# A two-layer hybrid mixer on one core: gates, first taps and modulation vectors moved between the input projection's chunks

## The chip, the cores and the metric

The kernel runs on one core of a Trainium2 chip. The metric is the device time of one execution in microseconds (us), here as the median of several runs. One core has five engines with an instruction stream each: TensorE (PE, matrix products; PEld is its weight load), VectorE (DVE), ScalarE (ACT), GpSimd (POOL) and SyncE (SP), whose queue issues most of the DMA loads. An engine takes its instructions in the order in which they are written, and waits on semaphores for the others.

## The reference, cut to what matters

256 context tokens and 256 latent tokens of width 1024 go through two layers. The part of a layer that the change touches:

```
mod = silu(c) @ w_mod[l] + b_mod[l]        # six vectors of 1024: sh1, sc1, gt1, sh2, sc2, gt2
h = rms_norm(x) * (1 + sc1) + sh1
a_val, a_gate, s_bg, s_cg, s_x, c_x, c_g = split(h @ w_in[l])       # 2304 columns
ya = silu(layer_norm(conv31(a_val * sigmoid(a_gate))))              # 256 channels
yb = s_bg * conv3(s_cg * s_x)                                       # 256 channels
xc = conv4(c_x) + lru_conv_b                                        # 512 channels
for d in (forward, backward):
    r = sigmoid(xc @ w_a[d] + b_a[d]); i = sigmoid(xc @ w_x[d] + b_x[d])
    log_a = 8 * r * log_sigmoid(lam[d])
    h_d = scan(exp(log_a), sqrt(1 - exp(2 * log_a)) * i * xc)
yc = (h_f + h_b) * gelu(c_g)
x = x + gt1 * (head_rms_norm([ya, yb, yc]) @ w_out[l])
x = x + gt2 * channel_mixer(...)            # layer 0: SwiGLU, layer 1: 2 of 8 SwiGLU experts
```

In layer 1 the context tokens are needed for `c_x` alone (for the scans' first states).

## The kernel before, in words

Activations lie transposed, channels on the partitions and the 512 tokens (layer 1: mostly the 256 latent ones) along the free axis. A product in fp32 accuracy is made of three products of a high and a low part: ScalarE copies a weight chunk of 1 MB into its high part (`hi`, L1464), VectorE takes the difference (`low`, L1896), and TensorE multiplies high by high, high by low and low by high.

`w_in` comes in nine chunks of 256 columns, in the order `WIN_ORDER` (0, 1, 4, 3, 2, 5, 6, 7, 8); this document calls them first to ninth chunk. Chunks 5 and 6 (sixth and seventh) are `c_x`, chunks 7 and 8 (eighth and ninth) are `c_g`. The third-next chunk's `hi` and `low` are made when a chunk's product ends.

After the ninth chunk comes what is called the interior here: the gates of the linear recurrence (RG-LRU), four tiles of 128 channels in each of two directions. Per tile TensorE makes two products of 512 columns (`bank<-xc,G`), ScalarE runs `gates(d, t)` (two tanh, exp, tanh, and outside the forward direction of layer 0 a square, L1611 to L1624), VectorE four or three operations (L2179 to L2188), ScalarE a square root (L1659), VectorE a product and a scan (L2209 to L2222). Between them stand the layer norm of the 31-tap convolution (its centring is L2196, its squares on ScalarE L1651) and the head norms (L1629 to L1640). Then the output projection `w_out` follows.

A modulation vector takes four chunks of `w_mod` of 1 MB and is read by TensorE straight from the ring buffer `raw` (`modulation`, 32 instructions, `bank<-raw,cc`). Before, all four vectors of a layer (gt1, sh2, sc2, gt2) are made in the interior. VectorE copies each out by `mod_row`.

The order of the work is written out by hand. Who does how many of the 62 taps of the 31-tap convolution when (L2059 first taps, L2062 the others) stands in the table `TAPS`; `CONF_AT` and `MEAN_AT` say after which gate tile the centring and the mean come. The DMA order is the list `CHUNKS`: the ring has five slots, so a chunk is loaded when the one five places before it has been used (a projection chunk: when its `low` is done). `mods_after` puts the `w_mod` chunks into that list.

At the start, small tables of parameters (`TABLES`) are transposed by TensorE into a bank and copied to `PT`, and `decay_rates` makes 8 log_sigmoid(lam) by 22 small operations on VectorE.

Of the kernel before, what the change touches and what calls it, by code (L numbers as in the profile page):

```python
# [29 lines left out]
P = 128  # L30
D = 1024
KD = D // P
NC = 256
# [181 lines left out]
def program(nc, a, out, known, marks):  # L215
# [5 lines left out]
    with ctx:  # L221
# [165 lines left out]
        MOD, STAT = bank[6], bank[7]  # L387

# [59 lines left out]
        def weights(c):  # L448
# [11 lines left out]
            if c[0] == "down":  # L460
# [12 lines left out]
        TAPS = {0: {"half": 2, 1: 8, 4: 13, 3: 11, 2: 13, 5: 4, 7: 11, 8: 0, "gate": 0},  # L473
                1: {"half": 3, 1: 3, 4: 5, 3: 7, 2: 21, 5: 0, 7: 4, 8: 7, "gate": 4}}
        BACK = (5, 6, 2, 3)

        CONF_AT = {0: 1, 1: 3}
        MEAN_AT = {0: 1, 1: 4}

        def mod_rows(l, q):  # L480

            b, half = {(0, 2): (4, 0), (0, 3): (4, 1), (0, 4): (5, 0), (0, 5): (5, 1),
                       (1, 0): (6, 1), (1, 1): (7, 0), (1, 2): (4, 0), (1, 3): (4, 1), (1, 4): (5, 0),
                       (1, 5): (5, 1)}[l, q]
            return bank[b][:, 256 * half:256 * half + 256]

# [283 lines left out]
        def _(pe):  # L770
# [10 lines left out]
            def tables(n):  # L781

                _, rows, _ = TABLES[n]
                return nc.tensor.transpose(STAT[:, P * n:P * n + rows], rows_sb[0:rows, n, :], ident[0:rows, 0:rows])
# [105 lines left out]
            def quarter_rows(c4):  # L890

                pe.wait_ge(dve_done, at("xT", "in", 4 + c4 % 2))
# [22 lines left out]
            def started():  # L915
# [7 lines left out]
                quarter_columns(0)  # L923
                for k in range(KD - 2):
# [19 lines left out]
                for t in range(2):  # L944
# [3 lines left out]
                    if t == 0:  # L948
                        pe.wait_ge(table_in, 16 * sum(len(parts) for parts, _, _ in TABLES[1:]))
                        pe.wait_ge(dve_done, at("t", 0, 1, KD - 1))  # L950
                        for m in range(1, len(TABLES)):
                            i = tables(m)
                        i.then_inc(pe_done, pe_n("tables"))
# [25 lines left out]
            for l in range(2):  # L979
# [7 lines left out]
                for c in WIN_ORDER[2:]:  # L987
                    project(("w_in", l, c), slice(0, T) if c in (5, 6) else ts, None)
                pe.wait_ge(gate_in, 8 * 16 * (l + 1))
                for q in range(8):  # L990
# [3 lines left out]
                    if q < 2:  # L994
                        pe.wait_ge(*evacuated(("w_in", l, WIN_ORDER[6 + q])))
                    else:
                        pe.wait_ge(act_done, at("gate_read", l, q - 2))
                    for w in range(2):
                        i = mm(bank[2 * (q % 2) + w][:, :], G[:, 8 * d + 4 * w + t, :], xc[:, t, :], True, True)
                    i.then_inc(pe_done, pe_n("gate", l, q))  # L1000
                    if (l, q) == (1, 3):
                        modulation(*MIX_MODS[l][0][0])
                    if q == CONF_AT[l]:
                        head_sums(l, ts, HEAD_SUM[0], (2, 3))
# [6 lines left out]
                    if (l, q) == (1, 4):  # L1011
                        modulation(*MIX_MODS[l][0][1], range(2))
                    if (l, q) == (0, 3):
                        modulation(*MIX_MODS[l][0][0])
# [9 lines left out]
                    if q == 5:  # L1024
                        modulation(*MIX_MODS[l][0][1], range(2 * l, MOD_K))
# [6 lines left out]
                modulation(*MIX_MODS[l][1][0])  # L1032
# [421 lines left out]
        def _(act):  # L1454
# [60 lines left out]
            for l in range(2):  # L1515
                ts = slice(lo[l], T)
                if l == 0:
# [25 lines left out]
                    for c4 in range(QUARTERS):  # L1543
# [5 lines left out]
                        if c4 == 0:  # L1549
                            hi(1)  # L1550
                    hi(2)
# [5 lines left out]
                for t in range(2):  # L1557
# [5 lines left out]
                    if l == t == 0:  # L1563
                        act.wait_ge(dve_done, at("lam_abs"))
# [1111 lines left out]
```

## Time and profile before

| what | us |
|---|---|
| three runs | 1555.26, 1559.27, 1558.04 |
| median | 1558.04 |
| the profiled execution | 1560.56 |
| its span | 1558.8 |
| its mean granted TensorE clock | 0.977 |
| busy: TensorE, VectorE, ScalarE | 1476.8, 838.1, 619.1 |

The page of the profile gives, of one execution, each engine's busy time and the span in 40 slices. The span is the time from the first to the last instruction; the profiled execution took 1.8 us more than its span. Because the engines' roles change from stage to stage, the shares of the whole span say little about one stage. The rows below are therefore read by stretch. Layer 0's first products start at 24.34 us, its ninth chunk ends near 135 us, its `w_out` starts at 188.81 us; layer 1's projection runs from 630 to 696 us and its `w_out` starts at 748.51 us. The experts fill the time from about 800 us on.

### The profile page before, as it was taken

The numbers are of one execution on the slowest core, as the hardware profiler recorded it, in microseconds if no ns is written. First come the engines' busy times: TensorE is split into PE (matmuls) and PEld (weight loads), VectorE is DVE, ScalarE is ACT, GpSimd is POOL, SyncE is SP. The second block draws the span as 40 slices with busy tenths as digits, with TensorE's granted clock in tenths as the row PEclk, the third lists the DMA queues.
The fourth block names the chain that finished last, engine by engine and source line by source line (L and its number), as shares of the span: only waits on it lengthen the run. The fifth ranks groups of instructions, "written<-read, shape, count | busy, mean of one in ns | idle before, by whom it ended". The sixth has DMA issues, their size and how long they took to land.

```text
span 1558.8 us, 21878 instructions
## 1 busy us (share of the span) xinstructions
PE 1476.8 (95%) x8674; PEld 1041.6 (67%) x8675; DVE 838.1 (54%) x1139; ACT 619.1 (40%) x702; POOL 18.2 (1%) x60
## 2 busy tenths in 40 slices
PE   6999698999999999896989999999999999999996
PEld 4886486788888887883855576565756566555754
DVE  4799944333333333898564554445645555445552
ACT  4426723232122232549253433434443444434442
POOL 2000000000000000000000000000000000000000
PEclk8999999999999999899989999999999999999998
DMA  9734914822543234349069999989999999999992
GB/s 330 228 108 163 350 60 158 216 61 75 135 109 91 74 92 135 109 135 347 6 266 389 341 327 332 342 329 401 385 408 405 404 384 402 408 356 402 384 409 88
DMA packets 214152, 395.47 MB, mean 254 GB/s; under 512 B 12044, under 2 KB 131232, under 8 KB 214048
## 3 DMA queue, kind: packets, MB, share of 16 engines
q1 hardware_dynamic: 213456, 393.80, 70.7%
q8 instruction: 74, 1.21, 0.3%
q10 hardware_dynamic: 592, 0.21, 0.1%
q14 instruction: 30, 0.25, 0.0%
HBM read 392.93 MB, written 1.05 MB: 253 GB/s over the span
## 4 chain that ended last, share of the span: by engine, by line
PE 84%; DVE 6%; ACT 5%; DMA 3%; issue 2%; DVEq 0%; SPq 0%; ACTq 0%
PE bank L772 82%; DMA raw<-in_moe_w 2%; DMA raw<-in_w_mod 1%; PE bank L1301 1%; ACT w_hi L1738 1%; DVE w_lo L2370 1%; DVE tb L1913 1%; ACT la L1617 1%; DVE lr L2222 1%; DVE y L2062 0%; DVE h_lo L1921 0%; ACT lr L1611 0%; PE bank L1246 0%; ACT lm L1659 0%; DVE li L2209 0%
## 5 line engine op out<-in xcount | busy, mean ns | idle before, releaser
L2370 DVE TENSOR_TENSOR w_lo<-raw,w_hi 128x2048 fp32r<-128x2048 f32 x132 | 302.4, 2291 | 266.2 <-ACT w_hi L1738 263.3
L1738 ACT ACTIVATE w_hi<-raw 128x2048 fp32r<-128x2048 f32 x132 | 252.3, 1912 | 406.2 <-PE bank L772 275.4
L772 PE MATMUL bank<-h_hi,w_hi 128*128 128x512 f32 (+1 forms) x768 | 285.7, 372 | 14.1 <-DVE h_lo L1921 12.0
L772 PE MATMUL bank<-h_lo,w_hi 128*128 128x512 f32 (+1 forms) x768 | 282.7, 368 | 0.0
L772 PE MATMUL bank<-h_hi,w_lo 128*128 128x512 f32 (+1 forms) x768 | 282.5, 368 | 0.0
L1464 ACT ACTIVATE w_hi<-raw 128x2048 fp32r<-128x2048 f32 (+1 forms) x64 | 113.7, 1776 | 195.7 <-PE bank L772 192.8
L772 PEld LDWEIGHTS bank<-h_hi,w_hi 128*128 128x128 f32 x768 | 146.7, 191 | 41.1 <-DVE h_lo L1921 13.9
L772 PEld LDWEIGHTS bank<-h_hi,w_lo 128*128 128x128 f32 x768 | 146.7, 191 | 23.8
L772 PEld LDWEIGHTS bank<-h_lo,w_hi 128*128 128x128 f32 x768 | 147.0, 191 | 23.0
L1896 DVE TENSOR_TENSOR w_lo<-raw,w_hi 128x2048 fp32r<-128x2048 f32 (+1 forms) x64 | 135.9, 2123 | 38.6 <-ACT w_hi L1464 38.5
L772 PE MATMUL bank<-w_hi,hc_hi 128*128 128x512 f32 (+1 forms) x384 | 153.6, 400 | 2.9 <-ACT warm L1793 2.9
L772 PE MATMUL bank<-w_lo,hc_hi 128*128 128x512 f32 (+1 forms) x384 | 144.7, 377 | 0.0
L772 PE MATMUL bank<-w_hi,hc_lo 128*128 128x512 f32 (+1 forms) x384 | 144.0, 375 | 0.0
L772 PE MATMUL bank<-raw,hcs 128*64 128x512 f32 (+2 forms) x736 | 116.7, 453 | 0.1
L772 PEld LDWEIGHTS bank<-w_hi,hc_hi 128*128 128x128 f32 x384 | 72.5, 189 | 48.3 <-issue 24.3
L2279 DVE TENSOR_TENSOR sq<-tb,bank 128x512 f32<-128x512 f32 x22 | 15.1, 687 | 125.3 <-ACT tb L1704 125.3
L772 PEld LDWEIGHTS bank<-w_hi,hc_lo 128*128 128x128 f32 x384 | 72.6, 189 | 14.3
L772 PEld LDWEIGHTS bank<-w_lo,hc_hi 128*128 128x128 f32 x384 | 72.7, 189 | 10.5
L772 PEld LDWEIGHTS bank<-raw,hcs 128*64 128x64 f32 x736 | 43.6, 137 | 48.8 <-issue 43.3
L1704 ACT ACTIVATE tb<-bank 128x512 f32<-128x512 f32 x22 | 13.1, 597 | 155.5 <-PE bank L772 155.5
L772 PE MATMUL bank<-w_hi,hd_hi 128*128 128x512 f32 x176 | 72.6, 412 | 0.0
L772 PE MATMUL bank<-w_lo,hd_hi 128*128 128x512 f32 x176 | 69.3, 394 | 0.0
(323 smaller groups left out, 1795.7 us busy)
## 6 DMA issues: line engine op xcount, KB each, us to landing
raw<-in_moe_w SPq DMA_DIRECT2D x220, 1024.0 KB, 9.4
raw<-in_w_mod SPq DMA_DIRECT2D x48, 1024.0 KB, 8.6
raw_x<-in_moe_w SPq DMA_DIRECT2D x44, 1024.0 KB, 9.4
raw<-in_ffn_w SPq DMA_DIRECT2D x44, 512.0 KB, 5.4
raw<-in_w_in SPq DMA_DIRECT2D x18, 1024.0 KB, 5.7
raw<-in_ffn_w SPq DMA_DIRECT2D x16, 704.0 KB, 4.8
raw<-in_w_out SPq DMA_DIRECT2D x8, 1024.0 KB, 5.5
x_in<-in_ctx SPq DMA_DIRECT2D x1, 1024.0 KB, 5.0
```

The costliest lines, as they stand in the source:

```text
L772: return nc.tensor.matmul(dst, lhsT, rhs, start=first, stop=last)
L1301: i = nc.tensor.transpose(bank[TURN_BANK][:, P * t:P * t + P], hid[:, p % 2, P * t:P * t + P], ident[:, :])
L1464: nc.scalar.activation(w_hi[:, s % SPL, 0:n], raw[:, POS[c] % RAW, 0:n], ACT.Copy)\
L1617: nc.scalar.activation(la[:, t, :], lr[:, t, :], ACT.Exp, scale=cln[:, k:k + 1], bias=cln[:, k:k + 1]).then_inc(act_done, act_n())
L1704: nc.scalar.activation(tb[:, i11 % 2, :], bank[2 * (s % 3)][:, :], ACT.Silu)\
L1738: nc.scalar.activation(w_hi[:, j % SPL, :], raw[:, E_SLOT[j], :], ACT.Copy)\
L1896: V.tensor_tensor(w_lo[:, s % SPL, 0:n], raw[:, POS[SPLIT[s]] % RAW, 0:n], w_hi[:, s % SPL, 0:n].bitcast(F32), ALU.subtract).then_inc(dve_ ...
L1913: i = V.scalar_tensor_tensor(tb[:, d % 2, tok(s)], xT[:, d, tok(s)], amp[:, l, w - 1, d, s:s + 1], STAT[:, tok(s)], ALU.mult, ALU.mult)
L2222: V.tensor_tensor_scan(lr[:, t, tok(s)][:, ::-1], la[:, t, tok(s)][:, ::-1], li[:, t, tok(s)][:, ::-1], lr[:, t, 0:1] if s else 0.0, ALU.m ...
L2279: V.tensor_tensor(sq[:, i11 % 2, :], tb[:, i11 % 2, :], bank[2 * (s0 % 3) + 1][:, :], ALU.mult)\
L2370: V.tensor_tensor(w_lo[:, j % SPL, :], raw[:, E_SLOT[j], :], w_hi[:, j % SPL, :].bitcast(F32), ALU.subtract).then_inc(dve_done, dve_n(name ...
```

## The change

It does these things, in both layers unless a layer is named:

- the tables are transposed before the first product, into bank 4, and copied and turned into decay rates by VectorE between the first quarters of the input (layer 0);
- ScalarE makes the first tap of three convolutions (`conf_tap` for one of two tiles, `sconv_tap`, `lru_tap`), which VectorE made before;
- modulation vectors gt1 and sh2 (numbers 2 and 3) are made after the fourth and after the fifth chunk instead of in the interior, and their `w_mod` chunks stand at those places in the DMA order; number 4 moves to where they were;
- the gates of tiles 0 and 1 of the forward direction are made by TensorE between the two halves of the eighth and of the ninth chunk, and ScalarE's and VectorE's part of them follows there; they use other buffers (`lru`);
- the tables `TAPS`, `CONF_AT` and `MEAN_AT` change: no tap is left for the time after the ninth chunk's product in layer 0, ten are left in layer 1; layer 0's mean and centring come after the fourth gate tile instead of the second.

The core of the diff:

```
 def mods_after(c):
+    if c[0] == "w_in" and c[2] in WIN_ORDER[2:4]:
+        l, q = MIX_MODS[c[1]][0][WIN_ORDER.index(c[2]) - 2]
+        return [(l, q, kq) for kq in range(MOD_K)]
     if c[0] == "w_in" and c[2] == WIN_ORDER[-1]:
-        return [(l, q, kq) for batch in MIX_MODS[c[1]] for l, q in batch for kq in range(MOD_K)]
+        return [(l, q, kq) for l, q in MIX_MODS[c[1]][1] for kq in range(MOD_K)]
...
-        TAPS = {0: {"half": 2, 1: 8, 4: 13, 3: 11, 2: 13, 5: 4, 7: 11, 8: 0, "gate": 0},
-                1: {"half": 3, 1: 3, 4: 5, 3: 7, 2: 21, 5: 0, 7: 4, 8: 7, "gate": 4}}
+        TAPS = {0: {"half": 2, 1: 11, 4: 13, 3: 16, 2: 16, 5: 4, 7: 0, 8: 0, "gate": 0},
+                1: {"half": 3, 1: 3, 4: 5, 3: 9, 2: 21, 5: 2, 7: 9, 8: 10, "gate": 0}}
-        CONF_AT = {0: 1, 1: 3}
-        MEAN_AT = {0: 1, 1: 4}
+        CONF_AT = {0: 3, 1: 3}
+        MEAN_AT = {0: 3, 1: 4}
...
                 quarter_columns(0)
+                pe.wait_ge(table_in, 16 * sum(len(parts) for parts, _, _ in TABLES[1:]))
+                for m in range(1, len(TABLES)):
+                    i = tables(m)
+                i.then_inc(pe_done, pe_n("tables"))
...
-                for c in WIN_ORDER[2:]:
+                for c in WIN_ORDER[2:7]:
                     project(("w_in", l, c), slice(0, T) if c in (5, 6) else ts, None)
+                    if c in WIN_ORDER[3:5]:
+                        if c == WIN_ORDER[3]:
+                            pe.wait_ge(dve_done, at("t", l, 1, KD - 1))
+                        modulation(*MIX_MODS[l][0][WIN_ORDER.index(c) - 3])
                 pe.wait_ge(gate_in, 8 * 16 * (l + 1))
-                for q in range(8):
+                for q, c in enumerate(WIN_ORDER[7:]):
+                    w, banks = take(("w_in", l, c))
+                    for t in range(2):
+                        for kk in range(KD):
+                            o = 256 * kk + P * t
+                            i = split_mm(banks[t][:, ts], (w[0][:, o:o + P], w[1][:, o:o + P]),
+                                         (h_hi[:, kk, ts], h_lo[:, kk, ts]), kk == 0, kk == KD - 1)
+                        if t:
+                            i.then_inc(pe_done, pe_n("mm", ORD["w_in", l, c]))
+                        elif q == 0:
+                            pe.wait_ge(dve_done, at("xc", l, 0))
+                            pe.wait_ge(*evacuated(("w_in", l, WIN_ORDER[6])))
+                            gate(0)
+                        else:
+                            pe.wait_ge(dve_done, at("xc", l, 1))
+                            pe.wait_ge(dve_done, at("mod_row", *MIX_MODS[l][0][1]))
+                            gate(1)
+                for q in range(2, 8):
...
                 for c in WIN_ORDER[2:]:
                     s = ORD[("w_in", l, c)]
                     b = bank[2 * (s % 3):2 * (s % 3) + 2]
+                    if c == 7:
+                        act.wait_ge(dve_done, at("clp"))
+                        gates(0, 0)
+                    if c == 8:
+                        gates(0, 1)
+                        gelu(7)
                     act.wait_ge(pe_done, at("mm", s))
                     hi(s + SPL)
+                    if c == 8:
+                        gelu(8)
...
+                    if c in (5, 6):
+                        act.wait_ge(act_done, act_n.n)
+                        for t in (2 * (c - 5), 2 * (c - 5) + 1):
+                            nc.scalar.activation(xc[:, t, :].rearrange("p (s w) -> p s w", s=2), cxp[:, t, :, 0:256],
+                                                 ACT.Identity, scale=colv("lru_conv_w", 16 * l + t),
+                                                 bias=colv("lru_conv_b", 4 * l + t))\
+                                .then_inc(act_done, act_n("lru_tap", l, t))
...
                     if c in (7, 8):
                         conf_taps(budget[c])
+                        gated_input(0, c - 7)
...
                 for d in range(2):
                     for t in range(4):
                         q = 4 * d + t
+                        if q >= 2:
+                            gated_input(d, t)
```

Three places show how instructions stand. On TensorE in layer 0, before, nothing but `xc,G` gate products stands between the ninth chunk's last product and the head sums (`sq,head_51`), and a whole vector (`raw,cc` x32) comes after the fourth tile:

```order
L772 MATMUL bank<-h_hi,w_lo 128x512
L772 MATMUL bank<-xc,G 128x512 x4
L772 MATMUL bank<-sq,head_51 32x128 x4
L772 MATMUL bank<-sq,head_51 16x128 x4
L772 MATMUL bank<-y,ones_d 128x512 x2
L772 MATMUL bank<-xc,G 128x512 x4
L772 MATMUL bank<-raw,cc 32x256 x32
L772 MATMUL bank<-xc,G 128x512 x2
```

In the changed kernel such a vector stands in the projection, between the last product of the fourth chunk and the first of the fifth (another follows the fifth chunk, and two `xc,G` instructions stand in the middle of the eighth and of the ninth):

```order
L786 MATMUL bank<-h_hi,w_lo 128x512
L786 MATMUL bank<-raw,cc 32x256 x32
L786 MATMUL bank<-h_hi,w_hi 128x512
L786 MATMUL bank<-h_lo,w_hi 128x512
...
L786 MATMUL bank<-h_hi,w_lo 128x512
L786 MATMUL bank<-xc,G 128x512 x2
L786 MATMUL bank<-h_hi,w_hi 128x512
```

Sixty-four `raw,cc` instructions and two gate tiles moved ahead of the ninth chunk's end.

On ScalarE in layer 0, before, the ninth chunk's `w_hi` and gelu (`cxp<-bank`) are followed by all four forward tiles (`lr`, `li`, `la`, `lr`), of which the first is shown:

```order
L1464 ACTIVATE w_hi<-raw 128x2048
L1589 ACTIVATE cxp<-bank 128x2x256 x2
L1611 ACTIVATE lr<-bank,PT 128x512
L1613 ACTIVATE li<-bank,PT 128x512
L1617 ACT_TABLE_LOAD
L1617 ACTIVATE la<-lr,cln 128x512
L1619 ACTIVATE lr<-lr,clp 128x512
```

Now tile 1 stands ahead of them, with its results in `tb`, `sx` and `y`, and the eighth chunk's gelu and its table load stand between:

```order
L1617 ACTIVATE tb<-bank,PT 128x512
L1619 ACTIVATE sx<-bank,PT 128x512
L1623 ACTIVATE y<-tb,cln 128x512
L1625 ACTIVATE tb<-tb,clp 128x512
L1636 ACT_TABLE_LOAD
L1636 ACTIVATE cxp<-bank 128x2x256
L1497 ACTIVATE w_hi<-raw 128x2048
L1636 ACTIVATE cxp<-bank 128x2x256
L1617 ACTIVATE lr<-bank,PT 128x512
L1619 ACTIVATE li<-bank,PT 128x512
L1623 ACT_TABLE_LOAD
```

Two of four tiles are ahead of the last `w_hi` of the projection, and the table load for exp stays in the interior.

On VectorE in layer 0, before, the centring (`y<-bank,y`) stands behind the second tile (whose last two operations are the first two rows) and ahead of the third:

```order
L2185 SCALAR_TENSOR_TENSOR li<-li,xc 128x512
L2188 TENSOR_SCALAR lm<-lm 128x512
L2196 SCALAR_TENSOR_TENSOR y<-bank,y 128x512 x2
L2179 TENSOR_TENSOR lm<-la 128x512
L2183 SCALAR_TENSOR_TENSOR lm<-lm,lr 128x512
```

Now tile 1 stands behind the projection's last `w_lo`, and the centring behind the fourth tile:

```order
L1963 TENSOR_TENSOR w_lo<-raw,w_hi 128x2048
L2188 TENSOR_TENSOR y<-y 128x512
L2192 SCALAR_TENSOR_TENSOR y<-y,tb 128x512
L2193 SCALAR_TENSOR_TENSOR sx<-sx,xc 128x512
L2195 TENSOR_SCALAR y<-y 128x512
...
L2193 SCALAR_TENSOR_TENSOR li<-li,xc 128x512
L2195 TENSOR_SCALAR lm<-lm 128x512
L2266 SCALAR_TENSOR_TENSOR y<-bank,y 128x512 x2
L2276 TENSOR_TENSOR sx<-y,sx 128x512
```

The centring moved behind two more tiles; ScalarE's squares of it still stand ahead of the square roots.

On SP's queue, the eight `w_mod` chunks of vectors 2 and 3 stood behind the first three `w_out` chunks; now four stand between the sixth and the seventh `w_in` chunk, and four between the seventh and the eighth.

## Rows read from the trace of the kernel before

**Rows 1.** Windows, layers 0 and 1: start:end, length, engines busy, clock, DMA, GB/s

```profile
56.14:134.88 78.74, 78.74 (x350) 65.19 (x348) 77.19 (x132) 24.41 (x26) 0.00 (x0) 1.00 0.37 119
134.88:188.81 53.93, 41.46 (x453) 21.69 (x452) 50.17 (x77) 46.22 (x70) 0.00 (x0) 0.94 0.87 308
642.64:696.40 53.76, 53.76 (x361) 49.99 (x362) 48.72 (x77) 23.39 (x27) 0.00 (x0) 1.00 0.43 138
696.40:748.51 52.11, 38.01 (x452) 19.63 (x451) 47.03 (x88) 45.16 (x74) 0.00 (x0) 0.90 0.75 283
715.00:720.00 5.00, 4.42 (x60) 2.06 (x56) 4.90 (x7) 4.53 (x10) 0.00 (x0) 1.00 1.02 407
```

**Rows 2.** Chain of waits, layer 0's interior: start, us, what

```profile
135.16 1.64 ACT w_hi L1464
...
139.22 1.28 ACT L1617
...
147.15 0.57 ACT lr L1611
...
149.71 1.04 ACT sq L1651 x2
...
156.01 0.58 ACT lr L1611
...
188.81 54.77 PE bank L772 x392
```

**Rows 3.** Chain of waits, layer 1's interior

```profile
696.48 1.92 ACT w_hi L1464
...
700.78 2.77 DVE y L2062 x7
...
719.06 0.58 ACT lr L1611
...
722.14 0.57 ACT lr L1611
...
748.51 11.52 PE bank L772 x141
```

**Rows 4.** Timeline of TensorE, layer 0: start, us, instruction, idle before

```profile
134.88 3.60 PE L772 MATMUL bank<-xc,G 128*128 128x512 f32 x8
...
145.21 3.66 PE L772 MATMUL bank<-raw,cc 128*32 128x256 f32 x64
...
157.23 1.07 PE L772 MATMUL bank<-raw,cc 128*32 128x256 f32 x16 [1.23 <-DMA raw<-in_w_mod]
...
176.90 1.13 PE L772 MATMUL bank<-sq,head 128*4 128x128 f32 x16 [7.80 <-ACT sq L1629]
```

**Rows 5.** Timeline of VectorE, layer 0

```profile
120.17 1.91 DVE L2089 TENSOR_SCALAR xc<-cxp,PT 128x512 f32<-128x512 f32 x4
...
144.62 0.69 DVE L2179 TENSOR_TENSOR lm<-la 128x512 f32<-128x512 f32 x1 [0.20 <-ACT lr L1619]
...
146.90 1.28 DVE L2196 SCALAR_TENSOR_TENSOR y<-bank,y 128x512 f32<-128x512 f32 x2
```

**Rows 6.** Timeline of VectorE, layer 1

```profile
709.73 0.69 DVE L2183 SCALAR_TENSOR_TENSOR lm<-lm,lr 128x512 f32<-128x512 f32 x1
...
711.27 1.67 DVE L2062 SCALAR_TENSOR_TENSOR y<-vp,PT,y 128x256 f32<-128x256 f32 x4
...
714.39 0.75 DVE L2196 SCALAR_TENSOR_TENSOR y<-bank,y 128x256 f32<-128x256 f32 x2
```

**Rows 7.** Timeline of ScalarE, layer 1, at the fourth chunk's end

```profile
657.42 1.92 ACT L1464 ACTIVATE w_hi<-raw 128x2048 fp32r<-128x2048 f32 x1 [3.30 <-PE bank L772]
```

**Rows 8.** SP's queue, layer 1, the issue behind the sixth chunk's `low`

```profile
657.31 0.37 SPq L541 DMA_DIRECT2D raw<-in_w_out  x1
```

**Rows 9.** DMA issues in that window: KB each, us to landing

```profile
raw<-in_w_out SPq DMA_DIRECT2D x1, 1024.0 KB, 5.8
```

**Rows 10.** Timeline of TensorE, the first product of layer 0

```profile
24.34 0.80 PE L772 MATMUL bank<-h_hi,w_hi 128*128 128x512 f32 x1 [5.31 <-DVE h_lo L1921]
```

More of the change, by code:

```diff
@@ L993, in _ @@
                         pe.wait_ge(dve_done, at("xc", l, t))
-                    if q < 2:
-                        pe.wait_ge(*evacuated(("w_in", l, WIN_ORDER[6 + q])))
+                    if q == 3:
+                        pe.wait_ge(*evacuated(("w_in", l, WIN_ORDER[7])))
                     else:
                         pe.wait_ge(act_done, at("gate_read", l, q - 2))
[L998 to L1003, printed above, removed]
+                    gate(q)
+                    if q == 3:
+                        pe.wait_ge(act_done, at("gate_read", l, 1))
                         head_sums(l, ts, HEAD_SUM[0], (2, 3))
@@ L1010, in _ @@
                         i.then_inc(pe_done, pe_n("conf_mean", l))
[L1011 to L1014, printed above, removed]
+                    if q == 3 + l:
+                        modulation(*MIX_MODS[l][1][0], range(2))
                     if q == 4:
@@ L1024, in _ @@
                     if q == 5:
-                        modulation(*MIX_MODS[l][0][1], range(2 * l, MOD_K))
+                        modulation(*MIX_MODS[l][1][0], range(2, MOD_K))
                     if q == 6:
@@ new lines, in gelu @@
+                def gelu(c):
+                    act.wait_ge(dve_done, at("xc", l, 3))
+                    s = ORD[("w_in", l, c)]
+                    for t in range(2):
+                        nc.scalar.activation(cxp[:, 2 * (c - 7) + t, lo[l] // NC:2, 2:2 + 256],
+                                             bank[2 * (s % 3) + t][:, ts].rearrange("p (s w) -> p s w", w=256),
+                                             ACT.Gelu_apprx_tanh)\
+                            .then_inc(act_done, act_n(*(("evac", s) if t else ())))
@@ L1641, in head_out @@
                         .then_inc(act_done, act_n("y_hi", l, i8))
[L1643 removed]
                 for d in range(2):
[L1645 removed]
+                    for t in range(2 - 2 * d, 4):
                         gates(d, t)
@@ L1936, in normed @@
                             low(1)
+                            dve.wait_ge(pe_done, at("tables"))
+                            for m in range(1, len(TABLES)):
+                                to_columns(m).then_inc(dve_done, dve_n(*(("PT",) if m == len(TABLES) - 1 else ())))
+                            halved()
+                        if c4 == 1:
+                            decay_rates()
                     low(2)
@@ L2148, in _ @@
                     elif c == 5:
-                        for k in range(SCONV_K):
+                        dve.wait_ge(act_done, at("sconv_tap", l))
+                        for k in range(1, SCONV_K):
                             for t in range(2):
```

185 lines of the change are left out of this document (93 added, 92 removed).

## The prediction

> **What bounds the kernel now.** I read three views in this order. First the windows by stage: in both projections TensorE is busy for the whole stretch, 78.74 of 78.74 us and 53.76 of 53.76, at full clock; in both interiors it is not, 41.46 of 53.93 us and 38.01 of 52.11, while ScalarE and VectorE are busy for nearly all of them [rows 1]. So the reader is to see two regimes that follow each other: TensorE sets the projection's end, ScalarE or VectorE the interior's. Second the chain of waits: it runs through ScalarE from 135.16 us to the end of layer 0's gates [rows 2], and in layer 1 through VectorE's taps at 700.78 us, then through ScalarE [rows 3]. Third the timelines: a modulation vector takes TensorE 3.66 us, two gate tiles 3.60 us, and at 176.90 us TensorE had stood idle for 7.80 us behind ScalarE's squares, although four vectors were made in that interior [rows 4]. Its work there is covered.
>
> **The projections.** The change puts two vectors and two gate tiles in front of the ninth chunk's end: 2 x 3.66 + 3.60 = 10.9 us of TensorE in each layer [rows 4], in the stretch where TensorE never waits [rows 1]. Nothing leaves that stretch, so layer 0's ninth chunk ends at 135.16 + 10.9 = 146.1 us.
>
> In layer 1 a wait on DMA is added. The latent projection's chunks last only 5.8 us each, and the ring makes loads late: the seventh `w_in` chunk used to be loaded far ahead, now its slot comes free with the sixth chunk's `low`, whose issue stands at 657.31 us [rows 8]. A load of that place took 5.8 us to land [rows 9]; alone I take 5, so it lands near 662.3. Its `w_hi`, which started at 657.42 us [rows 7], starts 5 us later. Vector 3's four chunks take the slots of vector 2's, freed from 658.4 on, and queue behind it. At 407 GB/s (the last window of [rows 1]) 1.05 MB take 2.6 us, so they land near 665, 667.6, 670.2 and 672.7. TensorE reaches vector 3 at 657.4 + 3.7 + 5.8 = 666.9 and would end at 670.5; behind the last landing it ends at about 673.3. That is 2.8 us of waiting. Bounds: 0, if transfers overlap as well as the 1.23 us that is layer 0's longest wait for them lets hope [rows 4]; and 10, if each batch is as late as twice a 5.8 us landing. I take 2.8, from the rate. The late seventh and eighth `w_hi` also hold ScalarE and VectorE, but their results are wanted from 684 us on. In layer 0 chunks last 10.9 us and the same sums end before TensorE asks: 0.
>
> **Layer 0's interior.** What leaves ScalarE's chain is two tiles at 149.71 - 147.15 = 2.56 us, 5.1 us [rows 2]. The table load of 1.28 us stays, since gelu stands between. From the ninth chunk's end, `w_hi` and gelu take 2.9 us, so tile 2 starts at 149.0 us, and its decay is ready 4.0 us later, at 153.0; tile 3's at 155.5. Before, the centring ran at 146.90 us, while ScalarE was still in the gates [rows 5]. Now it stands behind VectorE's part of tile 3: 155.6 + 2.28 (144.62 to 146.90 [rows 5]) = 157.9, and its first half ends at 158.5. ScalarE, done at 155.5, waits 3.1 us for it before the squares, and no other work is queued for it except what stands behind: square roots and the whole backward direction. From the squares to the first backward tile it was 156.01 - 149.71 = 6.3 us [rows 2], so that tile starts at 165.0 instead of 156.01: +9.0 us. Behind it nothing on the chain changes, and `w_out` starts near 197.8 instead of 188.81. VectorE's relief (four first taps of `xc` 1.91 us [rows 5], and a few more) lies in the projection, where VectorE isn't waited for, and the taps now ScalarE's lie where ScalarE is busy 24.41 of 78.74 us [rows 1]: 0 either way. Vectors 4 and 5 are made in less crowded interiors: 0.
>
> **Layer 1's interior.** The ninth chunk ends at 696.48 + 10.9 + 2.8 = 710.2. The gates of tile 1 are released only in the middle of that chunk, about 2.9 us ahead of its end; four activations (2.6), a table load and gelu (2.0) keep ScalarE until 711.9, so the last `w_hi` is 1.7 us late and ends at 713.9. VectorE then has `w_lo` (2.3), ten taps at 0.4 us (1.67 for four), tile 1 (2.3, with the square now VectorE's), tiles 2 and 3 at 711.27 - 709.73 = 1.54 us each, and the centring [rows 6]: 713.9 + 2.3 + 4.0 + 2.3 + 3.1 + 0.7 = 726.3. ScalarE is done with tile 3 at 722 and waits for it, as it did before. From the centring's end to the first backward tile it was 719.06 - 715.1 = 4.0 with the second half of the squares inside it; less what overlaps, the tile starts at 729.4 against 719.06: +10.4 us. The 19 taps that VectorE had there before are 10 now, and that with the two tiles of 722.14 - 719.06 = 3.08 us [rows 3] is what buys back 3.3 of the 13.7 us.
>
> **The start.** TensorE had stood idle for 5.31 us before the first product, waiting for VectorE [rows 10]; the three transposes go into that gap, and the table copies and decay rates into gaps in which VectorE waited for the next quarter. Between -0.5 (the transposes no longer stand between products) and +1.5 (the decay rates reach into the next quarter); I take -0.1.
>
> **The sum** against the profiled execution (1560.56 us, which is 2.5 above the median): +9.0 + 10.4 - 0.1 = +19.3 us, so 1579.9 there and 1577.3 on the scale of the median 1558.04. Its ends: with all waits of VectorE and DMA gone, the two tiles fully repaid and layer 1 bound by ScalarE alone, +5.8 and +5.0, together +11; with 10 us of DMA wait in layer 1 instead of 2.8 and some 2 for the start and for the clock, +28.5.
>
> **The clock.** The interiors have a granted clock of 0.94 and 0.90 [rows 1], that is, TensorE fell from 2.4 to 1.2 GHz in the idle time ahead of 176.90 us and came back after it. With one vector less there, that idle time grows from 7.80 to about 13 us [rows 4]. The work that follows until `w_out` is the same and lasts 12 us, in which the clock came back before, so I count 0, with 1 us a layer as the upper bound. The Trainium skill (TensorE: Matmul & The Clock Gate, the part on the clock gate) says that idle gaps throttle the engine and that this penalty is paid again each time. By that rule the added idle is harmful if the clock is still low when `w_out` starts; the trace agrees that it falls, and shows it back in time.
>
> **Rivals.**
> A, the other side: the interior is paced by the stream of `w_mod`. For it: DMA is busy 0.87 of layer 0's interior, and sixteen chunks of 2.6 us are 41 us of 54 [rows 1]. Eight of them leave for a stretch with a share of 0.37. Then each interior shortens by 8 x 2.6 = 20.5 us and each projection grows by 10.9, a gain of 9.6 a layer: 1558 - 19 = 1539. It decides if TensorE's wait for a chunk ends later than ScalarE's squares do. Against it: TensorE waited for a chunk 1.23 us, and 7.80 us for the squares with its vectors done [rows 4]. The Trainium skill (Perfetto Trace Analysis, Optimization Strategy) says that where the most contended engine changes over time, interleaving those regimes may help. That is what the change tries; by this rule the time would fall towards 1539 too, but the rows let only ScalarE's 5 to 6 us a layer be interleaved, while TensorE's work goes into the regime that TensorE bounds.
> B, cancelled: layer 0's centring isn't waited for (CONF_AT costs nothing), layer 1's DMA wait is 0, and VectorE's relief shortens more than ScalarE's chain: under +4.7 us in all. Against it is that even the two chains at their shortest leave +11: 1561.
> C, worse: layer 1's ring is late at every step (seventh chunk, vector 3, eighth chunk), and TensorE stands 10 us or more: 1588. For it is that the loads now follow use and not lie ahead; against it are 10.9 us chunks behind them in which to catch up.
>
> **Chances.** Forecast 0.75 (1568 to 1585); A 0.05; B 0.06; C 0.14. A measurement of this kernel tells about 0.3%, 4.7 us, from no change. So faster 0.05, the same 0.05, slower 0.90. The time is 1577, the range 1567 to 1587.
>
> **What would show it.** Right: in layer 0 the ninth chunk's `w_hi` starts near 146 instead of 135.16, the first backward tile near 165, `w_out` near 198; ScalarE idle some 3 us before the squares; in layer 1 a wait of TensorE for `w_mod` of 2 to 3 us before the sixth chunk, ninth chunk +13.7, `w_out` +10.4 against the layer's own start; TensorE's longest idle time in layer 0's interior 12 to 14 us. Wrong: a projection that grows by less than 10 us, or an interior shorter by more than 8 us, in which case ScalarE was not what set it.

## The result, and the profile after

The changed kernel takes 1582.44 us (median of 4 runs, 1578.33 to 1582.47) where the kernel before takes 1557.94: a ratio of 1.0153 [1.0132, 1.0174]. It is slower, as forecast, by 24.5 us where +19.3 were forecast (1577, range 1567 to 1587). Its profiled execution took 1578.33 us with a span of 1576.6; the other three have spans of 1580.7, and e0 takes up that difference.

The windows of its stages, columns as in [rows 1]: layer 0's projection from a `w_hi` near 56 us to the ninth chunk's, its interior up to `w_out`; then layer 1's projection from the third chunk's end to the ninth's, and its interior. (The projections' windows in [rows 1] begin at other events, 1.7 us earlier in layer 0 and 9 us in layer 1, so their lengths are not to be compared; the table below has both kernels from the same event.)

```profile
56.26:146.11 89.85, 88.90 (x479) 69.39 (x478) 76.20 (x105) 34.29 (x40) 0.00 (x0) 1.00 0.60 206
146.11:197.99 51.88, 33.92 (x317) 17.48 (x315) 42.67 (x62) 40.59 (x62) 0.00 (x0) 0.77 0.45 143
659.59:719.90 60.31, 56.14 (x422) 45.86 (x422) 45.35 (x75) 24.31 (x32) 0.00 (x0) 1.00 0.79 270
719.90:768.34 48.44, 30.09 (x318) 14.91 (x317) 43.22 (x77) 41.05 (x67) 0.00 (x0) 0.82 0.36 122
```

The reader is to see that layer 0's projection has grown by 12.3 us (from the same event, in the table below) and its interior has shrunk by only 2 against [rows 1], although TensorE has 7.5 us less to do there and DMA's share fell from 0.87 to 0.45. TensorE's work left a place where nobody waited for it. In both projections TensorE is now no longer busy all the time: 0.95 us idle in layer 0, 4.2 in layer 1.

The timeline of ScalarE in layer 0's interior, which answers to [rows 2]:

```profile
146.11 1.91 ACT L1497 ACTIVATE w_hi<-raw 128x2048 fp32r<-128x2048 f32 x1 [0.50 <-PE bank L786]
...
154.73 0.81 ACT L1625 ACTIVATE lr<-lr,clp 128x512 f32<-128x512 f32 x1
158.56 1.23 ACT L1718 ACTIVATE sq<-y 128x512 f32<-128x512 f32 x2 [3.02 <-DVE y L2266]
...
164.97 0.67 ACT L1617 ACTIVATE lr<-bank,PT 128x512 f32<-128x512 f32 x1
```

The ninth chunk's `w_hi` starts 10.95 us later than the 135.16 of [rows 2], the gates are done at 155.5, then ScalarE waits 3.02 us for the centring (L2266), and the first backward tile starts at 164.97. TensorE's rows in the two layers, which answer to [rows 4]:

```profile
125.91 1.98 PE L786 MATMUL bank<-xc,G 128*128 128x512 f32 x4 [0.95 <-DVE xc L2169]
138.62 1.88 PE L786 MATMUL bank<-xc,G 128*128 128x512 f32 x4
...
185.93 1.13 PE L786 MATMUL bank<-sq,head 128*4 128x128 f32 x16 [13.81 <-ACT sq L1697]
...
674.43 1.07 PE L786 MATMUL bank<-raw,cc 128*32 128x256 f32 x16
676.39 1.07 PE L786 MATMUL bank<-raw,cc 128*32 128x256 f32 x16 [0.89 <-DMA raw<-in_w_mod]
678.94 1.07 PE L786 MATMUL bank<-raw,cc 128*32 128x256 f32 x16 [1.48 <-DMA raw<-in_w_mod]
681.53 1.07 PE L786 MATMUL bank<-raw,cc 128*32 128x256 f32 x16 [1.52 <-DMA raw<-in_w_mod]
```

The idle time behind the squares has grown from 7.80 us [rows 4] to 13.81. In layer 1 vector 3 waits three times for its chunks, 3.89 us. The loads of `w_in` come late too. The first block below, from ScalarE's timeline, shows the `w_hi` of the seventh and the eighth chunk in layer 1, the first of which answers to [rows 7]. The second, from VectorE's timeline, shows such lateness in layer 0:

```profile
670.08 1.92 ACT L1497 ACTIVATE w_hi<-raw 128x2048 fp32r<-128x2048 f32 x1 [8.05 <-DMA raw<-in_w_in]
684.57 1.92 ACT L1497 ACTIVATE w_hi<-raw 128x2048 fp32r<-128x2048 f32 x1 [12.57 <-DMA raw<-in_w_in]
```

```profile
100.04 2.29 DVE L1963 TENSOR_TENSOR w_lo<-raw,w_hi 128x2048 fp32r<-128x2048 f32 x1 [4.43 <-ACT w_hi L1497]
...
122.47 4.05 DVE L2169 SCALAR_TENSOR_TENSOR xc<-cxp,PT,xc 128x512 f32<-128x512 f32 x6
126.44 2.28 DVE L1963 TENSOR_TENSOR w_lo<-raw,w_hi 128x2048 fp32r<-128x2048 f32 x1
```

The second block is a new feature of layer 0: VectorE stands idle for 4.43 us behind a late load, and then works without a gap until `xc`, for which TensorE waits 0.95 us.

Where the time went is read best by stage. This table, made from the traces of all kernels, has the time between named events: start (to the fourth `w_hi` of the timeline from 40 us on, at the third chunk's end), projection (from there to the ninth chunk's `w_hi`), interior (to the first product of `w_out`), middle (to the same third chunk of layer 1), projection and interior again, and the rest.

| kernel | start | proj. 0 | int. 0 | middle | proj. 1 | int. 1 | rest | ratio to before |
|---|---|---|---|---|---|---|---|---|
| before | 69.88 | 65.28 | 53.65 | 462.85 | 44.82 | 52.03 | 810.29 | |
| changed | 68.50 | 77.61 | 51.88 | 461.60 | 62.15 | 46.60 | 808.26 | 1.0153 [1.0132, 1.0174] |
| changed, again (e0) | 68.93 | 77.13 | 51.72 | 463.14 | 64.80 | 46.59 | 809.39 | 1.0167 [1.0153, 1.0181] |
| e1, vectors back | 69.34 | 74.50 | 51.74 | 462.86 | 50.05 | 46.73 | 808.78 | 1.0054 [1.0042, 1.0067] |
| e2, vectors only | 68.30 | 72.91 | 53.62 | 463.45 | 57.20 | 53.01 | 810.11 | 1.0143 [1.0127, 1.0158] |
| e3, centring early | 68.73 | 77.48 | 49.17 | 461.35 | 64.81 | 46.61 | 808.85 | 1.0145 [1.0131, 1.0160] |
| e4, gates late | 68.07 | 72.91 | 56.84 | 461.32 | 59.54 | 51.11 | 808.91 | 1.0160 [1.0144, 1.0176] |
| e5, e1 + tap table | 68.95 | 68.81 | 51.74 | 461.35 | 50.06 | 46.73 | 809.06 | 1.0007 [0.9998, 1.0016] |
| e6, three mends | 69.70 | 68.81 | 49.17 | 461.20 | 48.48 | 47.84 | 807.30 | 0.9999 [0.9989, 1.0010] |
| e7, layer 1 later | 69.53 | 77.35 | 51.73 | 463.28 | 60.29 | 46.60 | 809.72 | 1.0148 [1.0132, 1.0163] |
| e8, taps and tables | 68.91 | 65.28 | 53.64 | 462.74 | 44.55 | 54.05 | 808.33 | 1.0002 [0.9993, 1.0012] |
| e9, two mends | 69.24 | 68.82 | 49.17 | 463.60 | 50.06 | 46.67 | 809.64 | 0.9997 [0.9988, 1.0006] |

Start, middle and rest vary by 1 to 3 us between executions whatever the kernel. The other four columns repeat within 0.2 us where the code is the same (projection 0 of the changed code within 0.5), except projection 1 of kernels with its vectors early. Differences of 1 us in those four are read as real, smaller ones not.

### The profile page after: what moved, and what is told of

Same layout as the page of the kernel before. It is cut to its first block, busy times and chain, and to the rows that moved or that the text cites. A ratio compares the mean times of both kernels' runs of the same rounds, so it can differ in the third digit from the quotient of the medians.

```text
span 1576.6 us, 21881 instructions
## 1 busy us (share of the span) xinstructions
PE 1482.3 (94%) x8674; PEld 1042.5 (66%) x8675; DVE 834.0 (53%) x1125; ACT 628.6 (40%) x716; POOL 18.2 (1%) x60
## 4 chain that ended last, share of the span: by engine, by line
PE 83%; DVE 8%; ACT 4%; DMA 2%; issue 2%; POOL 0%; DVEq 0%; ACTq 0%; POOLq 0%
PE bank L786 81%; DVE y L2140 2%; DVE w_lo L1963 1%; DMA raw<-in_w_in 1%; PE bank L1334 1%; DMA raw<-in_w_mod 1%; DMA raw<-in_moe_w 1%; ACT w_hi L1497 1%; DVE tb L1980 1%; DVE h_lo L1988 0%; PE bank L1279 0%; PE bank L811 0%; DVE lr L2289 0%; ACT la L1623 0%; DVE y L2280 0%
## 5 line engine op out<-in xcount | busy, mean ns | idle before, releaser
L786 PEld LDWEIGHTS bank<-w_lo,hc_hi 128*128 128x128 f32 x384 | 72.4, 189 | 10.4
```

The source lines that it names most:

```text
L786: return nc.tensor.matmul(dst, lhsT, rhs, start=first, stop=last)
```

## The experiments

In the expectations a theory is what the run should show if my reading is right, and a rival what it should show if another is. The code cuts show the core of each edit; "..." marks what is left out.

**e1: the vectors back.** The rest of the change stays.

```
-    if c[0] == "w_in" and c[2] in WIN_ORDER[2:4]:
-        l, q = MIX_MODS[c[1]][0][WIN_ORDER.index(c[2]) - 2]
...
-                        modulation(*MIX_MODS[l][0][WIN_ORDER.index(c) - 3])
...
+                    if (l, q) == (1, 4):
+                        modulation(*MIX_MODS[l][0][1], range(2))
+                    if (l, q) == (0, 3):
+                        modulation(*MIX_MODS[l][0][0])
...
+                modulation(*MIX_MODS[l][1][0])
```

> The changed kernel with modulation vectors 2 and 3 back in the interiors, at the places of the kernel before; gates of tiles 0 and 1, first taps on ScalarE and early tables stay. Theory (TensorE sets the projection's end, so 2 x 3.66 us per layer are paid there, and layer 1 pays its 3.9 us of waiting for w_mod too): -7.3 in layer 0, less about 2.5 us in which TensorE now waits for VectorE's xc (which was ready at 126.4 us and comes some 5 us earlier without the late load, against TensorE being there at 119), and -7.3 - 3.9 in layer 1: about -16 us, so 1566 where the changed kernel has 1582. TensorE's wait for ScalarE's squares in layer 0's interior falls from 13.8 to 6 to 8 us. Rival A (the stream of w_mod chunks paces the interior): the interiors grow by as much as the projections shrink, or more: 1580 or above. Rival D (VectorE sets layer 0's projection, its taps stand ahead of xc): layer 0 gives back nothing, only layer 1's 11: 1571.

Measured: 1565.31 us beside 1556.20. The interiors didn't move (51.74 and 46.73 us against 51.88 and 46.60) although two vectors each went into them: rival A is dead. Layer 1's projection fell by 12.1 us. TensorE's wait for ScalarE's squares in layer 0 is 6.10 us. Layer 0's projection fell by only 3.1, less than my 4.8, and the timeline of TensorE says why:

```profile
121.92 3.67 PE L783 MATMUL bank<-xc,G 128*128 128x512 f32 x4 [3.74 <-DVE xc L2168]
```

and the windows just before and during that row:

```profile
118.00:121.92 3.92, 0.18 (x1) 0.00 (x1) 3.92 (x7) 0.00 (x0) 0.00 (x0) 1.00 0.00 0
121.92:128.50 6.58, 6.58 (x18) 4.03 (x19) 6.58 (x8) 2.68 (x4) 0.00 (x0) 0.74 0.41 121
```

TensorE waits 3.74 us for `xc`, and then the granted clock is 0.74, that is, the first part of the stretch is at 1.2 GHz: the same four matrix products take 3.67 us and not 1.98. The wait costs 3.7 and the clock behind it 1.7 or more.

**e2: the vectors alone**, on the kernel before.

```
+    if c[0] == "w_in" and c[2] in WIN_ORDER[2:4]:
+        l, q = MIX_MODS[c[1]][0][WIN_ORDER.index(c[2]) - 2]
...
+                        modulation(*MIX_MODS[l][0][WIN_ORDER.index(c) - 3])
...
+                    if q == 3 + l:
+                        modulation(*MIX_MODS[l][1][0], range(2))
```

> The kernel before with one part of the change alone: modulation vectors 2 and 3 made after the fourth and the fifth chunk, their w_mod chunks at that place in the DMA order, vector 4 in their place in the interior. Theory: +7.3 in layer 0, +7.3 and 3 to 4 us of waiting for w_mod in layer 1, nothing back from the interiors: +18, about 1576. Rival A (w_mod paces the interior): 1539 to 1545, below the kernel before. Rival D (VectorE sets layer 0's projection): layer 0 costs less than 7.3, since VectorE was busy 77 of 79 us there: +11 to +14 in all, 1570.

Measured: 1579.50 beside 1556.20, +23 where I expected +18. Projection 0 +7.6, interior 0 unchanged (53.62), projection 1 +12.4 with waits of 4.2 us for `w_mod`, interior 1 +1.0. These four stages sum to +21 us, 3 more than expected, nearly all of it in layer 1. The vectors alone make up nearly the whole loss. That e1, without them, is slower than the kernel before by 9 us all the same comes mostly from the wait for `xc`, which shows only when the vectors are gone (e5). Rival D fell for this kernel: VectorE, 77 of 79 us busy, did not hold the projection.

**e3: the centring early.**

```
-        CONF_AT = {0: 3, 1: 3}
-        MEAN_AT = {0: 3, 1: 4}
+        CONF_AT = {0: 2, 1: 3}
+        MEAN_AT = {0: 2, 1: 4}
```

> The changed kernel with layer 0's mean and centring after the third gate tile instead of the fourth. Theory (ScalarE waited 3.0 us for the centring with all else queued behind the squares): ScalarE goes straight from the gates to the squares, -2.6 us, first backward tile near 162.4 instead of 165.0. Rival (the centring only moved the wait: VectorE's part of the fourth tile, now later by the centring's 1.3 us, holds the square roots, or TensorE is late with the mean): 0 to -1.

Measured: interior 0 is 49.17 us, 2.7 less. The squares' row in the timeline of ScalarE, and the first backward tile:

```profile
156.10 1.23 ACT L1718 ACTIVATE sq<-y 128x512 f32<-128x512 f32 x2 [0.47 <-DVE y L2266]
...
162.51 0.67 ACT L1617 ACTIVATE lr<-bank,PT 128x512 f32<-128x512 f32 x1
```

The wait is 0.47 us where it was 3.02. The median is 3.0 us below e0's 1582.72; the kernel before, run beside each, was 0.7 lower beside e3.

**e4: the gates of tiles 0 and 1 late.**

```
-                        elif q == 0:
-                            pe.wait_ge(dve_done, at("xc", l, 0))
-                            pe.wait_ge(*evacuated(("w_in", l, WIN_ORDER[6])))
-                            gate(0)
...
+                for q in range(2):
+                    pe.wait_ge(dve_done, at("xc", l, q))
...
-                    for t in range(2 - 2 * d, 4):
+                    for t in range(4):
                         gates(d, t)
...
-                        gated_input(0, c - 7)
```

> The changed kernel with the gates of tiles 0 and 1 (TensorE's products, ScalarE's and VectorE's part) back behind the ninth chunk; buffers, vectors, taps and tables stay as changed. Theory: the projections shrink by 1.8 to 3.6 us each, layer 0's chain on ScalarE grows by 5.1 (+1.5 for the layer), layer 1's on VectorE by two tiles' parts but the last w_hi is no longer late (-1.9): -0.4 in all, so early gates are worth nothing here. Rival (early gates are what buys the interiors their time and only the vectors cost): +5 us or more per layer, 1592.

Measured: 1581.98 beside 1556.20, about the changed kernel's time. Projection 0 falls by 4.7 us (3.6 of products, 0.95 of waiting for `xc`) and interior 0 grows by 5.0; in layer 1 it is 62.15 + 46.60 = 108.75 against 59.54 + 51.11 = 110.65, or 0.7 less than e0's 111.39. So the gates are worth nothing that can be told from no change: what the interiors gain is what the projections lose.

**e0: the changed kernel once more.**

> The changed kernel once more, unedited, beside the others of this call, as their yardstick: 1.5% over the kernel before, 1580 where that has 1556. Its profiled execution was 4.1 us shorter than its three others; all theories expect a spread of some 4 us and, in the stages up to layer 1's w_out, the same durations within 0.5 us, since the four kernels with other edits differ from each other there only by their edits.

Measured: 1582.72 beside 1556.86 (five runs within 1.7 us). The spread that I expected of it didn't come: this execution has the long form, and my statement that the stages agree within 0.5 us is wrong for one of them, projection 1: 64.80 against 62.15 us. The rows of vector 3 in its timeline of TensorE, and two windows over and behind them:

```profile
678.06 1.07 PE L786 MATMUL bank<-raw,cc 128*32 128x256 f32 x16 [1.23 <-DMA raw<-in_w_mod]
680.90 1.83 PE L786 MATMUL bank<-raw,cc 128*32 128x256 f32 x16 [1.77 <-DMA raw<-in_w_mod]
683.48 1.94 PE L786 MATMUL bank<-raw,cc 128*32 128x256 f32 x16 [0.75 <-DMA raw<-in_w_mod]
```

```profile
680.90:688.00 7.10, 6.35 (x38) 3.32 (x39) 0.00 (x0) 1.48 (x1) 0.00 (x0) 0.52 1.08 351
688.00:697.82 9.82, 9.82 (x45) 8.12 (x44) 9.29 (x19) 1.77 (x5) 0.00 (x0) 1.00 1.09 359
```

The waits are nearly the same in sum (3.75 us), but here TensorE's clock falls to 1.2 GHz for some 7 us, and the projection takes 2.65 us longer. Of the five profiled executions with these waits, three show it (e0, e3 with 64.81, e4), two don't (changed, e2). So 2.65 of the 4.1 us between the first profile's span of 1576.6 and the other three of 1580.7 may be this. It isn't shown: those three have no trace, the start, the middle and the rest vary by as much, and e2's profiled execution, without the low clock, is the longest of its four.

**e5: eight taps behind `xc`.** On e1, one row of the table:

```
-        TAPS = {0: {"half": 2, 1: 11, 4: 13, 3: 16, 2: 16, 5: 4, 7: 0, 8: 0, "gate": 0},
+        TAPS = {0: {"half": 2, 1: 10, 4: 13, 3: 13, 2: 12, 5: 4, 7: 8, 8: 0, "gate": 0},
```

> As e1_mods_back (vectors in the interiors, gates early), and layer 0's tap table changed: 8 of the 62 taps move from ahead of xc to behind it (budgets 1: 10, 3: 13, 2: 12, 7: 8). Theory D' (in e1 TensorE waited 3.7 us for xc and 2.2 us for the second tile's, since VectorE makes 8 x 0.67 us of taps more ahead of xc than the kernel before does): these 5.9 us go, layer 0's ninth chunk comes 5 to 6 us earlier, w_out too, 1560. Rival (VectorE has no idle time in this stretch, so the taps only move the wait to the eighth or the ninth w_lo): gain 0 to 2 us, 1564.

(The 2.2 us that the expectation names are a wait for `mrow` in the interior, which I had misread; what the place costs beside the wait is the low clock. The taps are ahead of `xc` because the changed `TAPS` moved eleven there: `7: 11` became `7: 0`.) Measured: 1558.35 beside 1556.86, and projection 0 at 68.81 us, 5.7 less than e1. The timeline of TensorE:

```profile
117.63 1.88 PE L783 MATMUL bank<-xc,G 128*128 128x512 f32 x4
130.28 1.88 PE L783 MATMUL bank<-xc,G 128*128 128x512 f32 x4
```

No wait, no slow products; 68.81 - 65.28 = 3.53 us is what two gate tiles cost, near the 3.60 of [rows 4]. VectorE's later work found room; its timeline has these rows at the ends of the eighth and the ninth chunk:

```profile
127.14 2.29 DVE L1962 TENSOR_TENSOR w_lo<-raw,w_hi 128x2048 fp32r<-128x2048 f32 x1 [3.45 <-ACT w_hi L1496]
...
139.78 2.29 DVE L1962 TENSOR_TENSOR w_lo<-raw,w_hi 128x2048 fp32r<-128x2048 f32 x1 [2.78 <-ACT w_hi L1496]
```

It idles 3.45 and 2.78 us there, so the taps did not only move the wait, as the rival had it.

**e6: three mends.** e5, the centring of e3, and in layer 1

```
                         gates(0, 1)
-                        gelu(7)
+                        if l == 0:
+                            gelu(7)
                     act.wait_ge(pe_done, at("mm", s))
                     hi(s + SPL)
                     if c == 8:
+                        if l == 1:
+                            gelu(7)
                         gelu(8)
```

> As e5_taps_behind_xc, with two edits more: layer 0's mean and centring after the third gate tile (worth 2.7 us from the ninth chunk to w_out in e3), and in layer 1 ScalarE makes the last w_hi ahead of the eighth chunk's gelu, not behind it (it was 1.9 us late, VectorE stood idle 0.9 us for it). Theory: -2.7 and -0.9 against e5, 1556, no slower than the kernel before and within 0.3% of it. Rival (ScalarE is as much of a bound in layer 1's interior, and gelu behind w_hi costs there what w_hi gains): 1557 to 1559.

Measured: median 1554.50 beside 1556.86, but eleven runs lie in two groups (seven from 1553.84 to 1555.70, four from 1557.59 to 1560.44), and the ratio is 0.9999 [0.9989, 1.0010]: no difference from the kernel before (the means are 0.7 us apart, the medians 2.4). The third edit gained 1.6 us in projection 1 and gave back 1.1 in the interior, so by the stages the rival is mostly right about it.

**e7: layer 1's vectors two chunks later.**

```
-    if c[0] == "w_in" and c[2] in WIN_ORDER[2:4]:
+    n = 2 + 2 * c[1] if c[0] == "w_in" else 0
+    if c[0] == "w_in" and c[2] in WIN_ORDER[n:n + 2]:
...
+                    n = 3 + 2 * l
+                    if c in WIN_ORDER[n:n + 2]:
...
+                        if (l, c) == (1, 7):
+                            dve.wait_ge(pe_done, at("used", "mod", *MIX_MODS[l][0][1], MOD_K - 1))
+                            for m in MIX_MODS[l][0]:
+                                mod_row(*m)
```

> The changed kernel with layer 1's vectors 2 and 3, and their w_mod chunks, two chunks later: after the sixth and the seventh chunk, which last 10.9 us each and not 5.8. Theory (the 3.9 us of waiting for w_mod come from the short chunks, behind which the ring can't refill): that wait falls to under 1 us, layer 1's ninth chunk comes 3 to 4 us earlier against the layer's start, 1577. Rival (the loads are late because each waits for a slot's release, whatever the chunk lasts): 3 to 4 us of waiting again, 1580.

Measured: 1579.64 beside 1556.86. Each vector is one unbroken row of TensorE's timeline:

```profile
683.86 3.66 PE L787 MATMUL bank<-raw,cc 128*32 128x256 f32 x64
...
698.55 3.66 PE L787 MATMUL bank<-raw,cc 128*32 128x256 f32 x64
```

No wait for `w_mod`, and no low clock in these rows; the seventh and the eighth `w_hi` are no longer late. The short chunks were the cause. Projection 1 is 60.29 us, 4.5 less than e0 and 1.9 less than the changed kernel. A new wait of 2.36 us for `mrow`, ahead of the second gate tile, took the rest, together with the clock behind it, as the gates' row in TensorE's timeline and a window from there on show (1.96 us for these products and a clock of 1.00 in the changed kernel's projection):

```profile
715.11 2.51 PE L787 MATMUL bank<-xc,G 128*128 128x512 f32 x4 [2.36 <-DVE mrow L2044]
```

```profile
715.11:718.50 3.39, 3.39 (x10) 2.07 (x11) 3.39 (x10) 0.85 (x2) 0.00 (x0) 0.69 0.95 319
```

**e8: taps and tables alone.** `tables`, `decay_rates`, `conf_tap`, `sconv_tap` and `lru_tap` as changed; all vectors, gates, `TAPS` and `CONF_AT` in the place and size of before. The first of these, against the kernel before:

```
-                            if k == 0:
-                                i = V.tensor_scalar(out_v, cxp[:, t, :, k:k + 256], w,
-                                                    colv("lru_conv_b", 4 * l + t), ALU.mult, ALU.add)
...
+                            nc.scalar.activation(xc[:, t, :].rearrange("p (s w) -> p s w", s=2), cxp[:, t, :, 0:256],
+                                                 ACT.Identity, scale=colv("lru_conv_w", 16 * l + t),
+                                                 bias=colv("lru_conv_b", 4 * l + t))\
```

> The kernel before with only the rest of the change: tables transposed and decay rates made between the first quarters, first taps of the three convolutions by ScalarE (and other buffers for gate tiles 0 and 1). All vectors in the interiors, all gates behind the ninth chunk, tap tables and the centring's place as before. Theory (TensorE sets the projections, so VectorE's relief of some 5 us in each isn't waited for; the start is bound by the quarters): 0 in every stage, 1556 to 1558, within 0.3% of the kernel before. Rival (VectorE was busy for 77 of 79 us of layer 0's projection and ahead of the centring in layer 1, so its relief pays): 2 us or more below it, mainly from layer 1's interior.

Measured: 1558.91 beside 1557.45, ratio 1.0002 [0.9993, 1.0012]. Projection 0 is 65.28 us, to the hundredth that of before. VectorE is busy for 61.15 of these 65.28 us, 4.1 less than before. Neither early tables nor that relief are worth anything where TensorE sets the end. My 0 in every stage isn't right for interior 1, which is 2.0 us longer in this one profile. Rows of TensorE, first of the kernel before:

```profile
713.08 1.10 PE L772 MATMUL bank<-y,ones_d 128*128 128x256 f32 x4 [0.67 <-DVE y L2062]
714.11 1.93 PE L772 MATMUL bank<-raw,cc 128*32 128x256 f32 x32
```

and of e8, with a window from the first of them on:

```profile
713.16 1.10 PE L783 MATMUL bank<-y,ones_d 128*128 128x256 f32 x4 [2.62 <-DVE y L2135]
714.19 3.23 PE L783 MATMUL bank<-raw,cc 128*32 128x256 f32 x32
```

```profile
713.16:717.42 4.26, 4.26 (x47) 2.45 (x51) 4.22 (x8) 1.34 (x4) 0.00 (x0) 0.68 1.02 408
```

Counted from the last `w_hi`, the mean (`y,ones_d`) comes 1.44 us later: two squares, of tiles 0 and 1, are VectorE's there (0.72 us each). TensorE waits 2.62 us for it and not 0.67, its clock falls, and the products of a vector (`raw,cc`) behind it take 3.23 us instead of 1.93. ScalarE then waits 2.06 us for the sums instead of 0.44. So the traces put the 2.0 us down to the squares and the clock; no run changes the squares alone.

**e9: e6 without its third edit.**

```
-                        if l == 0:
-                            gelu(7)
+                        gelu(7)
```

> As e6_all_mended without its third edit: vectors in the interiors, gates early, 8 taps behind xc, layer 0's centring after the third gate tile; layer 1's last w_hi again behind the eighth chunk's gelu. Theory: the third edit was worth 0.5 us by e6's stages (1.6 us in the projection, 1.1 given back in the interior), so this kernel is 0.5 us slower than e6: 0 to 1 us below the kernel before, which nobody can measure. Rival (e6's lower median came from the third edit): 2.5 us above e6.

Measured: 1557.52 beside 1557.45, ratio 0.9997 [0.9988, 1.0006]. In the table the two layers' stages are 0.4 us longer than e6's, as expected; the medians are 3 us apart, as the rival has it. Since the two kernels' intervals against the kernel before overlap almost wholly, what e6's lower group of runs comes from stays open. No version was shown to beat the kernel before.

## Why the prediction was right, step by step

**The projections are TensorE's.** Right, and the main term. In layer 0, 2 x 3.66 us of vectors show as +7.6 in e2, two gate tiles as +3.53 in e5. Sum forecast 10.9 a layer; layer 0's `w_hi` came at 146.11, forecast 146.1. That agreement is partly luck: the start was 1.4 us shorter than in the profile of before and the projection 1.4 longer than forecast. 0.95 us of that are the wait for `xc`; 0.3 show in e2 too, whose two vectors cost 7.63 us and not 7.32; the rest is within this stage's spread. I had counted late loads in layer 0 at 0: TensorE waits for no `w_mod` there, but the 4.43 us that VectorE idles behind a late `w_in` are longer than TensorE's wait for `xc`, which by this is the late load's. And I had counted VectorE's work there at nothing ("lies in the projection, where VectorE isn't waited for"). e1 shows how near that was to being wrong: take the vectors out and `xc` is the bound.

**Interior 0.** Right in size and mechanism: first backward tile forecast 165.0, measured 164.97; the wait for the centring forecast 3.1 us, measured 3.02; `w_out` forecast 197.8, measured 197.99; TensorE's idle time forecast 12 to 14, measured 13.81. e3 took the wait away and the time came back, e4 returned the two tiles and the chain grew by 5.0 (forecast 5.1).

**Layer 1.** The mechanism was right (seventh load and vector 3 late, last `w_hi` 1.9 us late against 1.7), the size too small. Measured from its own start, `w_out` came 11.9 us later in the first profile and 14.5 in e0, against 10.4. Two terms were mis-sized. The wait for `w_mod` is 3.9 us instead of 2.8: TensorE starts on the second to fourth chunk 2.6 us apart, which is the forecast's rate, but on the last of them only 21.9 us after the layer's start, where I had it land at 21.0. And I counted 0 for the clock, with 1 us a layer as the bound, and looked for it in the interiors alone. There 0 was nearly right: from the squares' row to `w_out` it is 12.06 us against 11.91 in layer 0. In layer 1's projection the clock costs 2.65 us in e0, and three of five profiled executions show it.

**The start**: -0.1 forecast; the kernels with early tables have 68.07 to 69.70, but e2, which hasn't them, has 68.30. Nothing can be put down to the change.

**The sum**: +19.3 forecast. e0's profile gives, by stage, -0.95 + 11.85 - 1.93 + 0.29 + 19.98 - 5.44 - 0.90 = +22.9. The two layers account for 5.1 us more than forecast, 0.9 in layer 0 and 4.1 in layer 1 (2.65 of clock, about 1 of waiting, the rest mostly the vector in four pieces); the start, the middle and the rest together came out 1.5 us below the forecast, within their spread. So the 3.6 us between 19.3 and 22.9 look better than the layers were. Small slips of the working change nothing: eight chunks of 2.6 us are 20.8 us and not 20.5, and neither layer 1's +5.0 in the lower end nor the 0.9 us of overlap taken off ahead of 729.4 has a sum. **Rival A** is refuted by e1 and e2. **B** is refuted in each of its parts: the centring is waited for (e3), layer 1 waits for its loads (e2), and VectorE's relief is worth nothing (e8). Of **C** a part happened: its late ring is real, at 3.9 us and 2.65 of clock, not 10.

## What to carry to other kernels

Where engines take turns at being the bound, work moved from one stage to another is worth what it costs on the engine that bounds each: the same vector was free in the interior (e1) and cost 3.7 to 3.8 us in the projection (e7, e2). A helper engine that is 98% busy but not waited for is not the bound; but ask for whom the bounding engine would wait next, since taking one cost away can put that in its place (e1). And price a short wait on TensorE above its length, since the clock may fall behind it (e0, e1, e7).

## What the runs showed of the hardware

Waits of 0.89, 1.48 and 1.52 us, a little over 1 us of work between them, left TensorE's clock at 2.4 GHz in one execution; 1.23 and 1.77 us in another brought it to 1.2 GHz for some 7 us and made 2.65 us of loss out of the same code. Their length alone doesn't decide it, as the first two rows of vector 3 in e2 and then in e3 show:

```profile
675.65 1.07 PE L775 MATMUL bank<-raw,cc 128*32 128x256 f32 x16 [1.19 <-DMA raw<-in_w_mod]
678.22 1.07 PE L775 MATMUL bank<-raw,cc 128*32 128x256 f32 x16 [1.50 <-DMA raw<-in_w_mod]
```

```profile
674.12 1.07 PE L786 MATMUL bank<-raw,cc 128*32 128x256 f32 x16 [1.13 <-DMA raw<-in_w_mod]
676.69 1.82 PE L786 MATMUL bank<-raw,cc 128*32 128x256 f32 x16 [1.50 <-DMA raw<-in_w_mod]
```

e3's waits are no longer than e2's, and its second row is slow (granted clock 0.51 from 676.69 to 683 us) where e2's isn't (1.00 from 675.65 to 683). With single waits it is the same. 3.74 us in e1 brought the clock down (four products took 3.67 us instead of 1.98), and so did 2.36 us in e7 and 2.62 in e8; 2.54 us in the kernel before, in layer 1's interior, did not:

```profile
704.74 1.96 PE L772 MATMUL bank<-xc,G 128*128 128x512 f32 x4 [2.54 <-ACT li L1613]
```

The Trainium skill (TensorE: Matmul & The Clock Gate, Part 1) says that the recent activity of the array sets the clock. These rows agree, and show that waits of nearly the same length end at either level, in the same program too, with a difference of 2.65 us in one stage that a comparison of single runs would put down to an edit.
